# Query columns multiplied with unnormalised rows turned straight from X, in a two-layer hybrid encoder on one core

## The reference, cut to what matters

```python
def rms_norm(x, g):
    xf = x.astype(jnp.float32)
    y = xf * lax.rsqrt(jnp.mean(xf * xf, axis=-1, keepdims=True) + RMS_EPS)
    return (y * g.astype(jnp.float32)).astype(x.dtype)
...
# each layer:
#   h = RMSNorm(x)
#   one combined input projection of h -> columns partitioned into
#     [diff-attn q | k | v | ssd z | ssd xBC | ssd dt (2 directions) | gate_attn | gate_ssd]
#   branch A: differential attention (8 heads, two softmax maps per head, QK-norm, ...)
```

## Time and profile before

| what | value |
|---|---|
| median of 3 runs | 1752.48 us (1751.34 to 1753.69) |
| profiled execution: its time | 1752.03 us |
| profiled execution: its span | 1750.0 us |
| PE busy | 1694.3 us (97%) |
| DVE / ACT / POOL busy | 712.6 / 683.8 / 668.4 us |
| DMA | 528.47 MB, mean 302 GB/s |
| layer 0: first product starts | 16.99 us |
| layer 1: first product starts | 884.95 us |
| layer 0: product of block 2 starts | 41.32 us |
| layer 1: product of block 2 starts | 909.23 us |

### The profile page before, as it was taken

The page is one execution under the profiler, slowest core; times in us unless marked ns, Lnnn a source line. Parts: engine busy times, 40 slices in busy tenths (PEclk is TensorE's granted clock), DMA queues, the critical chain, the costliest instruction groups (busy, mean ns, idle before and its releaser), DMA issues.

```text
span 1750.0 us, 23255 instructions
## 1 busy us (share of the span) xinstructions
PE 1694.3 (97%) x8996; PEld 1059.0 (61%) x8996; DVE 712.6 (41%) x1341; ACT 683.8 (39%) x1541; POOL 668.4 (38%) x536
## 2 busy tenths in 40 slices
PE   8999999999999999898999999999999999998997
PEld 5889877787434444343378898777864444443343
DVE  5728788524222212121266387865241212222122
ACT  5565787754211111111156567877541111111111
POOL 6888776895000000000077987768930000000000
PEclk9999999999999999999999999999999999999999
DMA  6544312766999999999954452227569999999997
GB/s 253 210 181 156 145 49 104 292 278 241 374 420 428 428 427 427 428 427 427 414 221 160 179 193 97 97 97 316 219 258 415 427 428 426 428 428 427 428 425 299
DMA packets 47523, 528.47 MB, mean 302 GB/s; under 512 B 5128, under 2 KB 7944, under 8 KB 17200
## 3 DMA queue, kind: packets, MB, share of 16 engines
q1 hardware_dynamic: 47376, 526.89, 73.5%
q0 software_dynamic: 32, 0.02, 0.0%
HBM read 525.82 MB, written 1.06 MB: 301 GB/s over the span
## 4 chain that ended last, share of the span: by engine, by line
PE 66%; DMA 11%; DVE 9%; SPq 5%; ACT 5%; issue 3%; POOL 1%; DVEq 0%; ACTq 0%
PE PS L1250 18%; DMA view<-in_w_exp_down_dram 10%; PE PS L1279 9%; PE PS L834 8%; PE PS L836 8%; PE PS L835 8%; SPq L658 5%; DVE view L1932 5%; PE PS L1197 2%; PE PS L1183 1%; DVE view L1928 1%; PE PS L1041 1%; ACT view L1503 1%; PE PS L1184 1%; PE PS L822 1%
## 5 line engine op out<-in xcount | busy, mean ns | idle before, releaser
L2299 POOL TENSOR_TENSOR view<-view,view 128x512 fp32r<-128x512 f32 x448 | 580.2, 1318 | 552.7 <-DVE view L1834 466.7
L1250 PE MATMUL PS<-view,view 128*64 128x512 f32 x2048 | 454.5, 596 | 21.7 <-issue 21.0
L1391 ACT ACTIVATE view<-view 128x512 fp32r<-128x512 f32 x448 | 274.9, 632 | 151.7 <-PE PS L836 147.3
L1250 PEld LDWEIGHTS PS<-view,view 128*64 128x64 f32 x2048 | 152.3, 137 | 295.5 <-issue 291.7
L834 PE MATMUL PS<-view,view 128*128 128x512 f32 x704 | 285.2, 405 | 5.7 <-POOL view L2299 3.3
L836 PE MATMUL PS<-view,view 128*128 128x512 f32 x704 | 275.0, 391 | 0.0
L835 PE MATMUL PS<-view,view 128*128 128x512 f32 x704 | 274.8, 390 | 0.0
L1279 PE MATMUL PS<-view,stb 128*64 128x512 f32 x1024 | 230.4, 597 | 8.7 <-DMA view<-in_w_exp_down_dram 5.9
L2199 DVE SCALAR_TENSOR_TENSOR view<-PS,gcol,view 128x512 fp32r<-128x512 f32 x64 | 48.1, 751 | 446.0 <-ACT view L1701 445.8
L834 PEld LDWEIGHTS PS<-view,view 128*128 128x128 f32 x704 | 132.3, 188 | 33.4 <-issue 5.7
L1279 PEld LDWEIGHTS PS<-view,stb 128*64 128x64 f32 x1024 | 71.7, 136 | 132.4 <-issue 115.2
(11 more groups left out here) (254 smaller groups left out, 2027.0 us busy)
## 6 DMA issues: line engine op xcount, KB each, us to landing
view<-in_w_exp_up_dram SPq DMA_DIRECT2D x60, 2048.0 KB, 26.5
view<-in_w_mix_dram SPq DMA_DIRECT2D x56, 2048.0 KB, 7.6
view<-in_w_exp_gate_dram SPq DMA_DIRECT2D x56, 2048.0 KB, 28.6
view<-in_w_exp_down_dram SPq DMA_DIRECT2D x56, 2048.0 KB, 29.8
view<-in_w_exp_down_dram SPq DMA_DIRECT2D x32, 512.0 KB, 11.4
view<-in_w_exp_gate_dram SPq DMA_DIRECT2D x8, 1024.0 KB, 10.4
view<-in_w_exp_gate_dram SPq DMA_DIRECT2D x16, 512.0 KB, 32.5
view<-in_w_exp_up_dram SPq DMA_DIRECT2D x16, 512.0 KB, 15.4
```

The lines of the kernel that those rows point to most:

```text
L1250: ins = pe.matmul(bank(ph, name, j)[e * CAP:(e + 1) * CAP, :], xgT1[:, k, at + e * CAP:at + (e + 1) * CAP], slot8[expert_block(j, kind, e) ...
L1391: nc.scalar.activation(highs(chunk), weights(slot8, chunk), ACT.Copy).then_inc(*high_ready.up(ph))
L2299: g_.tensor_tensor(weights(low8, chunk), weights(slot8, chunk), highs(chunk), ALU.subtract).then_inc(*low_ready.up(ph))
```

## The change

At the start of each layer X itself, not XN, is turned (`raw_turn`, key `("rT", k)`) into `rawh` and `rawl`, which lie where `Xtok` comes later. Blocks 0 and 1 are multiplied with these. XN is still made, for all later blocks: the squares of X stand on ACT's queue behind the raw high parts and the casts of chunks 2 to 7, the reciprocal root and XN on DVE's queue behind the raw low parts, and the eight pairs of XN are turned (`row_turn`) behind the eight chunks of block 1, the first of them with a wait for `xn_ready`. `norm_rows` now uses `rsqrt_by_column` (each step as two instructions of 128x1) and adds `eps_raw`, the ε of the unscaled heads; `rsqrt(..., raw=True)` adds it in two instructions for two row tiles in place of one. POOL's wait for `xn_ready` is gone. Block 0 is loaded in quarters with semaphores of their own, the first ahead of everything; `rel` and `oh` are issued from ACT's queue; `keep_busy(24)` becomes `keep_busy(8)`; the bridge is gone; the head scales of layer 0 (L1756 to L1760) stand on DVE behind block 1's heads and no longer ahead of block 0's.

```diff
-    f = [(("hT", k), 4 + k % 4) for k in range(KD)]
+    f = [(("rT", k), 4 + k % 4) for k in range(KD)]
     for b in range(PB):
         f += [(("p", b, t), (2 * b + t) % 4) for t in range(TT)]
+        if b == 1:
+            f += [(("hT", k), 4 + k % 4) for k in range(KD)]
...
+                for part in range(QUARTERS):
+                    cols = slice(part * SLOT // QUARTERS, (part + 1) * SLOT // QUARTERS)
+                    sp.dma_start(slot8[0].rearrange("p k c -> p (k c)")[:, cols], blocks[0][:, cols]
+                                 ).then_inc(*first_loaded[part].up(ph))
+                    if l == 0 and part == 0:
+                        channel_vectors(0, ph)
+                        sp.dma_start(X, x.rearrange("b (t p) d -> p (b t) d", p=P)).then_inc(s_x, 16)
...
-                    keep_busy(24)
+                    keep_busy(8)
                     pe.wait_ge(s_tabc, 1)
-                pe.wait_ge(*xn_ready.at(ph, 2))
+                    pe.wait_ge(s_x, 16)
+
+                def raw_turn(k):
+
+                    if l:
+                        for t in range(TT):
+                            pe.wait_ge(*out_of(Phase(l - 1), "s", ALL_PAIRS - 1, t, 2 * k // KD))
+                    transpose2(ph, lambda t: X[:, t, k * P:(k + 1) * P], ("rT", k))
+
                 def row_turn(k):
 
+                    pe.wait_ge(*xn_ready.at(ph, 2))
                     transpose2(ph, lambda t: XN[:, t, k * P:(k + 1) * P], ("hT", k))
...
-                    product(ph, [("p", b, t) for t in range(TT)], b, 1, hTh, hTl,
-                            ahead=None if b else lambda k: pe.wait_ge(*out_of(ph, "hT", k)),
-                            behind=None if b else first_block)
+                    product(ph, [("p", b, t) for t in range(TT)], b, 1, *((rawh, rawl) if b < 2 else (hTh, hTl)),
+                            ahead={0: lambda k: pe.wait_ge(*out_of(ph, "rT", k)),
+                                   2: lambda k: pe.wait_ge(*out_of(ph, "hT", k))}.get(b),
+                            behind=(raw_turns, row_turn, None)[min(b, 2)])
...
-                if l + 1 < DEPTH:
-                    bridge(8)
...
+                    if raw:
+                        link(v.tensor_scalar(var[:, 0:n // 2], var[:, 0:n // 2], 1.0 / width, eps_raw[:, 0:1], ALU.mult, ALU.add))
+                        v.tensor_scalar(var[:, n // 2:], var[:, n // 2:], 1.0 / width, eps_raw[:, 1:2], ALU.mult, ALU.add
+                                        ).then_inc(*rs_in.up(ph))
...
+                for k in range(KD):
+                    low_of(rawh[:, k, :], rawl[:, k, :], ("rT", k), k + 1, vcol[:, G1 + k:G1 + k + 1])
+                norm_rows()
...
+                    if b == 0:
+                        for k in range(KD // 2, KD):
+                            low_row(k)
+                    if b == 1 and l == 0:
+                        head_scales(ph)
...
-                pool.wait_ge(*xn_ready.at(ph, 2))
                 low(0, 2 * CHUNKS)
```

More of the change, by code:

```diff
@@ L437, in encoder @@
         rs4 = sb("rs4", [P, 6, TT, GROUPS])
+        eps_raw = sb("eps_raw", [P, TT])
         r1 = sb("r1", [P, 12, TT])
@@ L809, in keep_busy @@
                     pe.matmul(PS[:, 3, :], identb[:, :], maskb[:, 0:1, :].to_broadcast([P, 4, P]),
[L810 to L815, removed]
                               start=True, stop=True, skip_group_check=True)
@@ L1402, in layer @@
                 vcol = vcols[l]
+                cast(ph, 0, 2)
+                if l == 0:
+                    act.wait_ge(s_tab, 1)
+                    nc.scalar.activation(rtab.rearrange("p a b -> p (a b)"), PS[0:HEADS, 7, :], ACT.Copy
+                                         ).then_inc(s_tabc, 1)
+                act.wait_ge(*columns_in.at(ph, 1))
+                for k in range(KD):
+                    high_of(ph, rawh[:, k, :], ("rT", k), vcol[:, G1 + k:G1 + k + 1])
+                    if k in (1, 3):
+                        cast(ph, 2 + k // 2, 1)
+                    if k >= KD // 2:
+                        cast(ph, HIGHS + k - KD // 2, 1)
                 if l == 0:
@@ L1433, in layer @@
                     nxt = (b + 1) * CHUNKS
-                    cast(ph, nxt, 2)
+                    if b == 0:
+                        act.wait_ge(*sumsq.at(ph, 2))
+                    if b == 1:
+                        for k in (5, 6):
+                            high_row(k)
+                            cast(ph, nxt + k - 5, 1)
+                        high_row(7)
+                    else:
+                        cast(ph, nxt, 2)
                     if b == 1:
@@ L1468, in layer @@
                         cast(ph, nxt + 5, 2)
+                    elif b == 0:
+                        high_row(0)
+                        for k in range(3):
+                            high_row(1 + k)
+                            cast(ph, nxt + 4 + k, 1)
+                        high_row(4)
                     elif b < PB - 1:
@@ L1827, in low_of, with norm_rows @@
                                            op0=ALU.mult, op1=ALU.subtract).then_inc(*drain(ph, *key))
-                def norm_rows(count, sums, done):
-                    dve.wait_ge(*sumsq.at(ph, sums))
-                    link(v.tensor_copy(st[:, 0:TT], small[:, 0:TT]))
-                    r = rsqrt(TT, count, D)
+                def norm_rows():
+                    dve.wait_ge(*sumsq.at(ph, 2))
+                    r = rsqrt_by_column(1, D)
                     for t in range(TT):
```

67 lines of the change are left out of this document (34 added, 33 removed).

## The result

The changed kernel takes **1767.92 us** (median of 4, 1767.66 to 1770.52), the kernel before 1752.22 beside it: ratio 1.0088, 95% interval 1.0076 to 1.0100. It is 15.7 us slower. The forecast was +6.9 (1759), with a range up to 1766: right in sign, less than half in size, and the time lies outside the range.

A forecast was written before the change was run, and what follows sets the result against it. PE bounds the mixers, PE and DMA the experts. Each layer pays 3.7 + 2.0 + 2.6 = 8.3 us; with the starts' gains layer 0 is +5.0, layer 1 +1.9: +6.9, forecast 1759 us, range 1752.5 to 1766.

The forecast's parts named there:

- the branch between the layers: PE leaving it between layers, formerly covered by the bridge, costs by estimate 0 to 1 us; 0.3 taken.
- Start of layer 1: Turning X instead of XN brings layer 1's first product earlier, to about 878.1: gain 6.5 us (5.9 to 6.9).
- Start of layer 0: First product at about 12.4 for 16.99, with earlier loads and fewer keep-busy matmuls: gain 4.3 us after 0.3 deducted.
- Wait for XN: PE stands at XN's first turn behind block 1's chunk 0: 3.7 us a layer (2.1 to 4.6).
- Rival (a): Ports shared with POOL don't matter for XN and the heads; costs at their low end, 1752 to 1756; chance 0.20.
- The turns: Eight more pairs of turns a layer on PE, 0.25 us each: 2.0 us a layer (1.8 to 2.3).
- Block 2's wait: From block 1's end to block 2, PE waits 2.6 us more a layer (2.4 to 2.9), behind the later `dtwh`.
- Head scales: In layer 0 they stand on DVE ahead of block 2's heads, which miss POOL's pause: 1.0 us (0 to 4).
- Rival (c): PE's clock halves after its new waits: 1.5 to 1.9 us for each of up to four, 1761 to 1766; chance 0.18.
- that distance: First product to block 2 in a layer: 32.6 us forecast against 24.3 before; 26 or less would refute the forecast.

The follow-up runs named there:

- e2: Changed kernel with five of the eight unread bridge matmuls put back between the layers: 1765.81 us.
- e6: Changed kernel with PE leaving out, in layer 0 alone, the branch to the code for tokens over capacity: 1762.97 us, ratio 1.0061.
- e10: Changed kernel without layer 0's branch on PE, with 13 unread matmuls ahead of XN's turns and 5 ahead of the heads' transposes: 1758.59 us, ratio 1.0031.
- e4: Changed kernel with POOL's wait for XN put back, ahead of its 11th low part of the layer: 1765.38 us, ratio 1.0072.
- e11: As e10, plus POOL waiting for XN ahead of its 11th low part, and 8 unread matmuls for 13: 1756.23 us, ratio 1.0021.
- e5: Changed kernel with unread matmuls in all three idle times: 13 ahead of XN's turns, 11 ahead of the heads' transposes, six between layers: 1764.91 us.
- e1: Changed kernel with 13 unread PE matmuls ahead of the wait for XN in both layers: 1765.86 us, ratio 1.0079.
- e3: Changed kernel with both edits of e1 and e2: 13 unread matmuls ahead of the wait for XN and five bridge matmuls: 1765.53 us.
- e7: Kernel before with only its eight unread bridge matmuls between the layers taken out: 1756.66 us, ratio 1.0021.

## Why the prediction was wrong

Two steps failed: the price of the branch between the layers, taken as 0.3 us and measured at 5.2, and the clock, kept out of the sum as a rival at 0.18. The other terms came out within 1 us. In the prediction's order:

- **Start of layer 1, 6.5 us: 1.5 measured.** This is the step that failed first. Its number is "the branch between layers, which the bridge covered and no row prices, costs by estimate 0 to 1 us; I take 0.3": it is 5.2 us (e2, e6), which also gave the clock a place to fall. With it gone the gain is 6.9 (e6, e10). The prediction knew that a row was missing, and bounded the cost from nothing; the only bound that the rows gave was the cover itself, 7 us, and that should have been the upper end.
- **Start of layer 0, 4.3 us: 3.9 measured**, within its bounds. `oh` landed 4.9 us after its issue, as it had behind X. By the Trainium skill (SBUF — State Buffer, The DMA setup-cost knee), with its fixed 2 us and the bytes, it would have been there at about 3.5, an estimate; it was there at 6.12. The keep-busy matmuls were misread a little: eight of them, not nine, fill the 3.39 us ahead of 11.85 (a weight load runs one matmul ahead), 0.42 each, and the eight of after took 3.39.
- **Wait for XN, 3.7 us a layer: 2.99** (bounds 2.1 to 4.6). The pair took 2.6 (taken as 3.0). Rival (a) falls: e4 shows POOL's part.
- **The turns, 2.0 us a layer**: a chunk with a pair of turns takes 1.60 us (40.47 to 42.07), one without 1.36: 0.24 a pair, 0.25 taken.
- **Block 2's wait, 2.6 us: 2.8**. From the end of block 1's last product to block 2 it is 3.98 us in both layers of after, e6, e10 and e11, for 1.22 before. The path is the forecast one: `dtwl` begins at 45.16, POOL's first low part for block 2 follows it, and block 2 begins 2.65 us behind `dtwl`'s start (2.68 in before). The heads' transposes, let go by DVE's last low parts, end at 47.68 and so tie with that low part. Where they came later, as in e5, they set block 2's start.
- **Head scales, 1.0 us: 1.0.** From block 2 to the last product of layer 0's mixer it is 384.4 to 384.9 us in all nine versions of the change, and 383.3 to 383.8 in the four of the kernel before: means 384.58 and 383.54. In layer 1, which has no head scales, after, e1, e10 and e11 take 383.7 to 383.9, as the four do (383.6 to 383.8). No run moves the head scales alone.
- **Rival (c), the clock.** It was there with 1.5 to 1.9 us for each wait and a chance of 0.18. Its mechanism was right (PE idle, half the clock behind it), its price too low and its place incomplete: it had the clock fall after the two waits, not between the layers, where PE was to have none. e10 against after gives t0 to block 2 with and without the low clock: 2.6 us in layer 0 (34.72 - 32.10, one stretch of 5.9 us), 4.2 in layer 1 (36.32 - 32.08, two stretches). From layer 1's first turn to its first product it is another 0.3 (1.88 for 1.63 in e6). The argument against it was that no row showed so short an idle time doing this. The rows didn't, but the trace of before did, outside the mixers. In the experts' parts PE idles 2.54 to 2.56 us four times, and behind one of them the clock is at half (timeline, then window, of before):

```profile
1599.46 4.34 PE L1250 MATMUL PS<-view,view 128*64 128x512 f32 x12 [2.55 <-issue]
1599.20:1602.60 3.40, 3.14 (x8) 1.14 (x10) 0.00 (x0) 0.00 (x0) 0.00 (x0) 0.50 1.01 429
```

The sum mended, for the two profiled executions: forecast 6.9, the branch 5.2 less the 0.3 taken, the clock 2.6 + 4.2 + 0.3 = 7.1, the start of layer 0 less good by 0.4, t0 to block 2 with the clock held 32.1 for the 32.6 forecast, twice: 6.9 + 4.9 + 7.1 + 0.4 - 1.0 = 18.3, for 18.8 between the spans. The medians differ by 15.7, since after's profiled execution is 2.6 us above the median of its runs. By the medians the branch's 4.9 and the 4.4 that e10 gains on e6 make 16.2 of the 6.9, for 15.7 measured. e1 to e3 show that how often and where the clock falls is not the same in each execution. "If that distance is 26 or less, the forecast is wrong": the distance was 34.7 and 36.3 for the 32.6 named, and 32.1 with the clock held.

That e10 lands near 6.9 has some luck in it. Its profiled execution is 4.0 us above before's: the starts gave 11.1 us (10.8 forecast), t0 to block 2 cost 7.8 a layer (8.3), block 2 to layer 0's last product 1.9 (1.0), and the last stretch of the program was 2.4 shorter, which no term foresaw. The median's interval is 4 us wide.

What stays open: what decides, execution by execution, behind which idle time the clock falls, how much of e3's small gain is due to that, and what PE does in the 5.2 us.

## What to carry to other kernels

Matmuls that nobody reads may be cover for something that isn't in any row: before counting them as time to be won, give what lies under them the whole length of the cover as its upper bound. A wait put into PE's queue costs more than its length, because the clock behind it may be at half; price it as the wait and half of the stretch that follows (here 2.1 to 2.6 us a stretch). Where the wait can't be had away, put harmless work ahead of it, and ahead of the next wait too: filling one of them alone often moved the loss to the next. Look through the whole trace of before for idle times of that length, not only through the stage that is changed. And of a change with several parts, run the part that adds no wait alone: here only the earlier start of the program was worth having.

## What the runs showed of the hardware

- PE's granted clock was at half (1.2 GHz, 0.50) behind every idle time of 2.98 us or more in the layer starts of these profiles: behind 2.99 us six times (after, e2, e6), behind 5.2 us three times (after, e1, e4) and behind 6.91 once (e7). It was there when PE went on, or at most 0.8 us later, and stayed for 3.1 to 5.9 us of PE's work. At the heads' wait, 2.53 to 2.56 us, it fell in six of twelve cases, at most 1.7 us behind the wait's end (never in after, once each in e1, e2, e4 and e6, both times in e3), and behind 1.75 to 1.79 us in none of three. At half clock a pair of turns took 0.69 us for 0.44 behind the same wait, a product's matmul 0.63 for 0.39.
- PE needs 5.2 us (5.19, 5.21, 5.21 in after, e1 and e4) from its last matmul ahead of a branch not taken, over a long body of code, to the first one behind it, with nothing to wait for; without the branch 0.04 us (e6). ACT, whose queue has such a branch too, lost nothing that the trace shows: its first cast of layer 1 (882.57 in after) is ahead of PE's last product.
- A pair of DVE instructions on 128x1024 takes 1.42 us with POOL still (before, e4) and 2.60 to 2.63 beside it (after 2.61, e1 2.63, e6 2.60), while the chain of small 128x1 instructions (22.95 to 27.00, 4.05 us) is as long beside POOL as it was in the earlier trace rows.
- The first matmuls of the program run at half pace, 0.42 us for 0.21, until 10.2 to 13.6 us, where the trace's clock record begins with the full clock; the view's 1.00 ahead of that is no measurement.
